# First units of a chunk scan prepared inside the projection's last item

## The chip, the cores and the metric

The kernel runs on one core of one Trainium2 chip. The metric is the device time of one execution in microseconds (us), as the median of several runs. TensorE is called PE in the profile, VectorE DVE, ScalarE ACT, GpSimd POOL and SyncE SP; ACTq and SPq are the instruction queues of ScalarE and SyncE that issue transfers.

## The reference

One step of a diffusion backbone with one layer, in float32, over 1024 sample tokens and 128 prompt tokens (nine chunks of 128). RMSNorm and modulation, one input projection of 1024 to 3600 columns, two head groups side by side, an output projection, then a gated convolutional MLP. The first group is a Hyena long convolution (four blocks of 128 channels). The second is an mLSTM with 4 heads of 128, scanned by chunks in two directions (d = 0 forward, d = 1 backward):

```python
def step(carry, xs):
    C, n, m = carry
    b = jnp.cumsum(lfc, axis=-1)
    dmat = jnp.where(causal, b[..., :, None] - b[..., None, :] + ic[..., None, :], -jnp.inf)
    inter = b + m[..., None]
    m_t = jnp.maximum(inter, jnp.max(dmat, axis=-1))
    s = einsum('bhtd,bhsd->bhts', qc, kc) * jnp.exp(dmat - m_t[..., None])
    w_inter = jnp.exp(inter - m_t)
    num = einsum('bhts,bhse->bhte', s, vc) + w_inter[..., None] * einsum('bhed,bhtd->bhte', C, qc)
    den = jnp.sum(s, axis=-1) + w_inter * einsum('bhd,bhtd->bht', n, qc)
    ...
    C_new = w_c * C + einsum('bhs,bhse,bhsd->bhed', w_s, vc, kc)
```

The prompt's scan starts from zero, the sample's from the inputs state_mlstm_C, n and m. Outputs are both token sets and the prompt's final states.

## The kernel before, in words

The program is a row of phases. A phase is a block in which each engine has a program of its own, written out by hand, with semaphores between them; all engines meet at a barrier at its end. Two phases matter here.

**The projection** (`project_and_hyena`, lines 398 to 1580) runs 32 items, one after another on TensorE. Each product is made in three passes (high x high, high x low and low x high part of float32, lines 231 to 235). Items 20 to 31 are "tokens" items: three token groups of 24 matmuls each, evicted by ScalarE (line 1294) to one of two stage buffers and stored by SyncE (`store`, line 723). Items 23 to 28 are the values v, 29 to 31 part of the output gate o, whose eviction is a Sigmoid. Beside the items run other works, tied to item numbers: the way back of the Hyena convolution (`transform_back`; `finish(c)` on VectorE, lines 1413 to 1428, makes block c from loads of hv and x0, issued by `load_block`, and SyncE stores it, `store_block`); the gates of the mLSTM (`gate_parts` on VectorE, `gate_exponents` on ScalarE, `gate_transfers` on SyncE); and at item 28 the output weights: ScalarE weighs them (lines 1319 to 1323) and takes the high part of the second half (line 1324), GpSimd the low part (line 991).

The gates end in rows that the scan needs spread over all partitions. At item 29, after VectorE's steps at lines 1510 to 1515, ScalarE makes four exponents (lines 1256 to 1259). SyncE then writes the rows to DRAM in 16 small stores (line 864), 2 for the output new_m (line 866), stores item 29 and the last Hyena block, and `load_rows_and_values` (line 815) loads them back, broadcast to 128 partitions (512 KB a unit: the tops and the inter weights, for the first 4 units), waits for the stores of items 27 and 28, and loads the values of the first 5 chunks (256 KB each, line 826). Item 30's store stands behind these. GpSimd, when mask and all 4 rows are there, makes the masked tops of units 0 and 1 (line 995). In the last item, n = 31, between its first and second token group, TensorE waits for the gates' diagonal (VectorE, line 1519, behind `finish(3)`) and for the last block, and transposes the gate columns (lines 1149, 1150). ScalarE issues the loads of the initial state behind item 30 (lines 1316 to 1318), in rows by value.

**The scan** (`chunk_scan`, lines 2176 to 2519) has 18 units (d, chunk, s, update): units 0 and 1 are the prompt's chunk in both directions (s = 0, zero state), then the sample's chunks alternate, forward from 0 and backward from 7. Units 2 to 9 meet a chunk for the first time. For a unit n:

- SyncE loads keys and queries of a chunk (`load_chunk`), and rows into a ring of 4 (`load_rows`);
- GpSimd adds the mask to the rows (`masked(n + 1)`, line 2386), then weights the queries (line 2398) and the values (line 2406);
- ScalarE takes exponentials (`decays`, line 2436, two units ahead) and copies transposed keys (`copy_keys`, line 2416);
- TensorE makes the scores (line 2328, one unit ahead), transposes the keys of a new chunk (line 2334), makes the numerators (line 2363 with the values, line 2364 with the state) and the state's update (line 2375);
- VectorE multiplies scores by decays (`probabilities`, line 2480), updates the state (line 2497) and makes the output (lines 2508 to 2516).

Ahead of the loop TensorE makes scores(0), transposes the first keys and the initial state (`turn_state`, line 2337), ScalarE makes decays(0), the key copy, decays(1) and the state's copies, VectorE probabilities(0).

## Time and profile before

| | us |
| --- | --- |
| median of 3 runs | 1619.41 |
| lowest and highest | 1618.31, 1622.28 |
| the profiled execution | 1622.19 |
| its span, first to last instruction | 1620.3 |
| projection's last item ends, scan's first product | 554.0, 564.39 |
| scan's last instructions, next phase's first product | 640.2, 640.90 |

Times in the rows below are microseconds from the span's start. A bracket at a row's end is the idle time of that engine ahead of it and what ended it. A row with xN merges N instructions of one line.

### The profile page before, as it was taken

To read this page: it belongs to the slowest core of one execution; us is meant where nothing else is said; L and a number is where in the kernel's file an instruction comes from. 1 tells how busy PE (TensorE), PEld (TensorE's weight loads), DVE (VectorE), ACT (ScalarE), POOL (GpSimd) and SP (SyncE) were. 2 spreads that over 40 slices of the span, in tenths; PEclk is the share of its full clock that TensorE was granted. 3 is DMA by queue.
4 is the path that set the end of the run, shared out by engine and by line. 5 is a ranking of instruction groups with operands and counts; after the bars stand their busy time and mean duration, and the time that the engine had idled before them with its cause. 6 is when DMAs were issued, how large, how long until landed. Compare 5 with 4: busy or idle time off the path is not lost.

```text
span 1620.3 us, 22641 instructions
## 1 busy us (share of the span) xinstructions
PE 1551.0 (96%) x9583; PEld 1431.7 (88%) x9583; DVE 988.4 (61%) x1369; ACT 487.4 (30%) x696; POOL 472.7 (29%) x212
## 2 busy tenths in 40 slices
PE   5889999999999798999899999999999999999997
PEld 1477899999999798999799999999999999999996
DVE  5657134788325457415788638855883787288846
ACT  2574123222442367434422102211221122022203
POOL 1665213211311286053323213222232221232210
PEclk9899999999999899999999999999999999999999
DMA  9753423433636786410101011010110101101102
GB/s 348 287 215 114 180 70 111 176 143 109 218 112 219 243 263 208 131 46 7 53 26 53 27 53 48 32 52 27 53 53 27 53 26 53 53 27 53 42 24 117
DMA packets 111207, 168.09 MB, mean 104 GB/s; under 512 B 6395, under 2 KB 88451, under 8 KB 105987
## 3 DMA queue, kind: packets, MB, share of 16 engines
q1 hardware_dynamic: 107983, 163.72, 29.4%
q10 hardware_dynamic: 3124, 2.93, 0.6%
q8 instruction: 76, 1.25, 0.3%
q14 instruction: 24, 0.20, 0.0%
HBM read 135.35 MB, written 31.27 MB: 103 GB/s over the span
## 4 chain that ended last, share of the span: by engine, by line
PE 57%; DVE 3%; ACT 1%; issue 0%; POOL 0%; ACTq 0%; DVEq 0%
PE psum L231 19%; PE psum L233 18%; PE psum L235 18%; DVE mlp_acc_a L3199 1%; DVE tail_scan_h L3079 1%; PE psum L3303 0%; PE psum L3463 0%; DVE mlp_h_lo L3085 0%; DVE w_raw L3268 0%; DVE mlp_h_lo L3073 0%; DVE mlp_acc_a L3268 0%; DVE tail_x L3223 0%; DVE mlp_h_lo L3130 0%; ACT tail_x L2976 0%; PE psum L3334 0%
## 5 line engine op out<-in xcount | busy, mean ns | idle before, releaser
L231 PE MATMUL psum<-mlp_h_hi,w_hi 128*128 128x384 f32 (+2 forms) x1248 | 305.3, 340 | 6.5 <-DVE mlp_acc_a L3199 3.5
L233 PE MATMUL psum<-mlp_h_lo,w_hi 128*128 128x384 f32 (+2 forms) x1248 | 301.3, 337 | 0.0
L235 PE MATMUL psum<-mlp_h_hi,w_lo 128*128 128x384 f32 (+2 forms) x1248 | 301.1, 336 | 0.0
L3199 DVE SCALAR_TENSOR_TENSOR w_raw<-psum,par,w_raw 128x945 f32<-128x945 f32 (+2 forms) x176 | 214.7, 1220 | 91.8 <-ACT w_raw L3020 88.0
L3199 DVE SCALAR_TENSOR_TENSOR mlp_acc_a<-psum,par,mlp_acc_a 128x945 f32<-128x945 f32 (+2 forms) x176 | 214.5, 1219 | 33.1 <-ACT mlp_acc_a L3020 29.9
L2791 POOL TENSOR_TENSOR w_lo<-w_raw,w_hi 128x2048 fp32r<-128x2048 f32 x32 | 148.1, 4627 | 288.4 <-ACT w_hi L2785 288.4
L231 PEld LDWEIGHTS psum<-mlp_h_hi,w_hi 128*128 128x128 f32 x1248 | 205.7, 189 | 25.5 <-issue 6.3
L233 PEld LDWEIGHTS psum<-mlp_h_lo,w_hi 128*128 128x128 f32 x1248 | 206.6, 189 | 15.3
L235 PEld LDWEIGHTS psum<-mlp_h_hi,w_lo 128*128 128x128 f32 x1248 | 206.3, 189 | 15.4
L3223 DVE SCALAR_TENSOR_TENSOR tail_x<-psum,mod,tail_x 128x384 f32<-128x384 f32 (+1 forms) x192 | 94.8, 515 | 128.3 <-PE psum L235 128.1
L233 PE MATMUL psum<-tail_g_lo,w_hi 128*128 128x384 f32 x480 | 160.3, 334 | 0.0
L235 PE MATMUL psum<-tail_g_hi,w_lo 128*128 128x384 f32 x480 | 160.3, 334 | 0.0
L231 PE MATMUL psum<-tail_g_hi,w_hi 128*128 128x384 f32 x480 | 160.3, 334 | 0.0
L231 PE MATMUL psum<-head_big_hi,w_hi 128*128 128x384 f32 (+3 forms) x578 | 146.6, 334 | 1.2 <-issue 1.2
L235 PE MATMUL psum<-head_big_hi,w_lo 128*128 128x384 f32 (+3 forms) x578 | 144.0, 330 | 0.0
L233 PE MATMUL psum<-head_big_lo,w_hi 128*128 128x384 f32 (+3 forms) x578 | 144.0, 330 | 0.0
L2894 POOL TENSOR_TENSOR tail_g_lo<-mlp_acc_a,tail_g_hi 128x1152 fp32r<-128x1152 f32 x20 | 53.8, 2690 | 250.4 <-ACT tail_g_hi L3033 250.4
L946 POOL TENSOR_TENSOR w_lo<-w_raw,w_hi 128x2048 fp32r<-128x2048 f32 (+1 forms) x13 | 60.3, 4639 | 195.6 <-ACT w_hi L1173 195.6
L231 PEld LDWEIGHTS psum<-head_big_hi,w_hi 128*128 128x128 f32 x578 | 97.9, 190 | 13.0 <-issue 6.5
L235 PEld LDWEIGHTS psum<-head_big_hi,w_lo 128*128 128x128 f32 x578 | 97.7, 190 | 7.2
L233 PEld LDWEIGHTS psum<-head_big_lo,w_hi 128*128 128x128 f32 x578 | 97.7, 190 | 7.1
L2785 ACT ACTIVATE w_hi<-w_raw 128x2048 fp32r<-128x2048 f32 x32 | 61.1, 1908 | 127.6 <-PE psum L235 127.6
(390 smaller groups left out, 2490.4 us busy)
## 6 DMA issues: line engine op xcount, KB each, us to landing
w_raw<-ffn_w_up SPq DMA_DIRECT2D x22, 1024.0 KB, 5.1
filt_ada<-ada_w SPq DMA_DIRECT2D x16, 1024.0 KB, 9.9
w_raw<-w_in SPq DMA_DIRECT2D x13, 1024.0 KB, 5.8
w_raw<-ffn_w_down SPq DMA_DIRECT2D x11, 1024.0 KB
scan_spread<-scratch_scan_rows SPq DMA_DIRECT2D x18, 512.0 KB, 5.9
rownorm_ada<-ada_w SPq DMA_DIRECT2D x8, 1024.0 KB, 6.7
rownorm_x<-x_sample SPq DMA_DIRECT2D x8, 512.0 KB, 5.4
scratch_kt<-kt_spec SPq DMA_DIRECT2D x4, 1024.0 KB, 3.8
```

What stands on the lines that cost most here:

```text
L231: ins = nc.tensor.matmul(out, wh, x_hi(k, i), start=begin, stop=False)
L233: ins = nc.tensor.matmul(out, wh, x_lo(k, i), start=False, stop=False)
L235: ins = nc.tensor.matmul(out, wl, x_hi(k, i), start=False, stop=end)
L946: nc.gpsimd.tensor_tensor(weight_part("lo", u), raw(u), weight_part("hi", u).bitcast(F32), ALU.subtract)\
L2785: nc.scalar.activation(w_hi[:, u % 2, :], w_raw, ACT.Copy).then_inc(w_hi_done, 1)
L2791: nc.gpsimd.tensor_tensor(w_lo[:, u % 2, :], w_raw, w_hi[:, u % 2, :].bitcast(F32), ALU.subtract).then_inc(w_lo_done, 1)
L2894: nc.gpsimd.tensor_tensor(lo, acc_a[:, j, :], hi.bitcast(F32), ALU.subtract).then_inc(g_lo_done, 1)
L3079: ins = stt(out=hacc[:, c, h, :], in0=hacc[:, c, h, :], scalar=ss[:, c, h:h + 1], in1=o[:, h, chunk_at(t)], op0=ALU.mult, op1=ALU.mult)
L3199: ins = stt(out=out, in0=image(up_at)[:, r0 + dy:r1 + dy, c0 + dx:c1 + dx], scalar=weight(i, loc, t), in1=out, op0=ALU.mult, op1=ALU.add)
L3223: ins = stt(out=out, in0=src[:, a:z], scalar=gate[:, j:j + 1], in1=out, op0=ALU.mult, op1=ALU.add)
```

## The change

Five things are done.

1. Into the projection's last item. TensorE, at the place where it transposes the gate columns, also transposes the first chunk's keys and makes its scores, once for units 0 and 1; all into banks 0 to 2, which item 30 has left, so that the wait for the last Hyena block (`finished`) moves from TensorE to VectorE. ScalarE, ahead of the last item's eviction, makes the decays of units 0 and 1 and the key copy; VectorE the probabilities of both. The scan begins with these in place.
2. ScalarE issues the five value loads, at item 28, ahead of the weighing of the output weights; it waits for the stores of items 27 and 28, and SyncE therefore stores item 28 first in that item.
3. SyncE loads rows for 3 units ahead (instead of 4), for units 0 and 1 only the tops (256 KB each); GpSimd's tops wait for those two and the mask. Item 30's store goes ahead of these loads, the new_m stores behind them.
4. The initial state is laid out by key in the kernel's input (a transposition of the input array), so one load in the scan puts C and n in place, and its transposes and copies go. Unit 3's rows are loaded in the scan. The SyncE order there is: second chunk, state, rows of unit 3, third and fourth chunk.
5. Units 0 and 1 leave out the product with the zero state and the weighting of its queries; some semaphores are shared.

```diff
@@ SyncE, projection @@
-            def load_rows_and_values():
-                sp.wait_ge(rows_out, 16 * (4 * HEADS + 2))
-                for n in range(SCAN_ROWS):
+            def load_first_rows():
+                sp.wait_ge(gate_out, 16 * (ENDS + STARTS + 4 * HEADS))
+                for n in range(ROWS_AHEAD):
                     d, c, s, up = SCAN_UNITS[n]
-                    src = dram["scan_rows"][d, c:c + 1]...
+                    parts = 2 if s else 1
+                    src = dram["scan_rows"][d, c:c + 1, 0:parts]...
...
+                if n == 28:
+                    store(n)
                 if 26 <= n < 29:
                     store_block(n - 26)
...
                 if n == 30:
                     store_block(CH - 1)
-                    load_rows_and_values()
-                if kind(n) in STORED:
+                if kind(n) in STORED and n != 28:
                     store(n)
+                if n == 30:
+                    load_first_rows()
+                    for d in range(2):
+                        sp.dma_start(io["new_m"]...)
@@ GpSimd, projection @@
-            pool.wait_ge(scan_rows_in, 16 * (1 + SCAN_ROWS))
+            pool.wait_ge(scan_rows_in, 16 * (1 + READY))
@@ TensorE, projection, last item @@
-                        pe.wait_ge(finished, CH)
+                        pe.wait_ge(evac, count(n - 1, "tokens"))
...
+                        pe.wait_ge(scan_in, 16 * 2)
+                        for h in range(HEADS):
+                            nc.tensor.transpose(ps[:, 1, ...], ahead["first_k"][:, h, :], mem["ident"][:]).then_inc(first_products, 1)
+                        for h in range(HEADS):
+                            nc.tensor.matmul(ps[:, 0, ...], ahead["first_k"][:, h, :], ahead["first_q"][:, h, :], ...)
@@ ScalarE, projection @@
+                if n == len(items) - 1:
+                    act.wait_ge(columns_made, 1)
+                    for i in range(READY):
+                        act.wait_ge(first_top, i + 1)
...
+                            ins = nc.scalar.activation(ahead["decay"][:, i, h, :], ahead["top"][:, i, h, :], ACT.Exp, ...)
+                    act.wait_ge(first_products, 1 + HEADS)
+                    act.wait_ge(y_out, 16 * (CH - 1))
+                    nc.scalar.activation(ahead["k_tok"][:, 0], ps[:, 1, :]..., ACT.Copy)
                 act.wait_ge(product_done, n + 1)
...
-                if n == 30:
-                    act.wait_ge(finished, CH)
-                    for d in range(2):
-                        act.dma_start(ahead["c_rows"][d], io["state_mlstm_C"]...)
-                    act.dma_start(ahead["n_rows"], io["state_mlstm_n"]...)
+                if n == 28:
+                    for i in range(27, 29):
+                        j = count(i, *STORED) - 1
+                        act.wait_ge(stored[j % ST], 32 * (j // ST + 1))
+                    act.wait_ge(back, 1 + 2 * CH)
+                    act.wait_ge(y_lo_done, 1 + 2 * CH)
+                    for c in SCAN_ORDER[0:VALUES_AHEAD]:
+                        act.dma_start(ahead["v"][:, c, :, 0:HD], dram["v"][c]...).then_inc(values_and_rows_in, 16)
                 if n == 28:
                     act.wait_ge(w_out_in, 32)
@@ VectorE, projection, last item @@
+                    dve.wait_ge(first_products, 1 + 2 * HEADS)
+                    dve.wait_ge(finished, CH)
+                    for i in range(READY):
+                        dve.wait_ge(first_decay, i + 1)
+                        tt(ahead["prob"][:, i], ps[:, 0, :]..., ahead["decay"][:, i], ALU.mult)
@@ SyncE, scan @@
-            for c in order[1:4]:
+            load_chunk(order[1])
+            sp.dma_start(C[:, 1], io["start_by_key"]...).then_inc(state_in, 16)
+            for n in range(ROWS_AHEAD, RB):
+                load_rows(n)
+            for c in order[2:4]:
                 load_chunk(c)
@@ TensorE, scan @@
-            scores(0)
-            turn_keys(order[0], 1)
-            turn_state()
             for n in range(N):
-                if n + 1 < N:
+                if READY <= n + 1 < N and n >= READY:
                     scores(n + 1)
...
+                    nc.tensor.matmul(wide(num, h), prob[:, n % 2, h, :], v[:, c, h, :], start=True, stop=not s)
+                    if s:
+                        ins = nc.tensor.matmul(wide(num, h), qw[:, n % 2, h, :], C[:, s, 4 * d + h, :], start=False, stop=True)
                 ins.then_inc(num_done, 1)
-                if n == 0:
-                    pe.wait_ge(c_copied, 3)
+                if n == READY - 1:
+                    scores(READY)
+                    turn_keys(units[READY][1], B_S + (READY - 1) % 2)
```

## Rows read from the trace of the kernel before

**Rows 1.** Stretches: length, busy of PE, PEld, DVE, ACT, POOL, clock, DMA share, GB/s.
```profile
554.00:557.00 3.00, 0.00 (x0) 0.00 (x0) 0.00 (x0) 0.81 (x1) 0.00 (x0) 0.92 1.00 351
...
564.30:573.30 9.00, 8.91 (x54) 8.59 (x55) 2.30 (x3) 6.72 (x18) 7.54 (x7) 0.67 0.90 275
573.30:585.00 11.70, 11.70 (x108) 11.70 (x106) 7.67 (x28) 6.38 (x24) 7.96 (x8) 1.00 1.05 328
```
**Rows 2.** Timeline of TensorE: start, us, engine, line, operation [idle before <- releaser].
```profile
547.58 0.49 PE L1149 MATMUL psum<-ident,front_gates 128*128 128x128 f32 x3
...
564.39 2.04 PE L2328 MATMUL psum<-scan_first_q,scan_first_k 128*128 128x128 f32 x8 [10.42 <-PEq L259]
...
573.30 1.05 PE L2328 MATMUL psum<-tail_x 128*128 128x128 f32 x8
...
577.31 1.05 PE L2328 MATMUL psum<-tail_x 128*128 128x128 f32 x8
...
587.20 0.60 PE L2334 MATMUL psum<-ident,tail_x 128*128 128x128 f32 x4
```
**Rows 3.** Timeline of GpSimd, from 533 to 585.
```profile
533.28 4.62 POOL L991 TENSOR_TENSOR w_lo<-w_raw,w_hi 128x2048 fp32r<-128x2048 f32 x1 [35.16 <-ACT w_hi L1324]
559.80 0.16 POOL L993 MEMSET scan_v<- 128x36 f32 x1 [21.91 <-DMA scan_spread<-scratch_scan_rows]
...
575.59 1.27 POOL L2386 TENSOR_TENSOR scan_top<-scan_spread,scan_mask 128x512 f32<-128x512 f32 x1 [0.56 <-DMA scan_spread<-scratch_scan_rows]
...
582.28 1.27 POOL L2386 TENSOR_TENSOR scan_top<-scan_spread,scan_mask 128x512 f32<-128x512 f32 x1 [3.18 <-DMA scan_spread<-scratch_scan_rows]
```
**Rows 4.** Waits of SyncE's queue around the barrier: total us, times, longest.
```profile
SPq L259 <- DMA scan_v<-scratch_v: 2.5, 1, 2.5
```
**Rows 5.** Timeline of ScalarE, items 28 to 31 and the scan's start.
```profile
527.93 3.32 ACT L214 ACTIVATE w_raw<-w_raw,par 128x256 f32<-128x256 f32 x8 [2.17 <-PE psum L235]
...
538.63 0.40 ACT L1256 ACTIVATE front_gates<-front_gates,hyi_gate_small 128x128 f32<-128x128 f32 x1 [5.42 <-DVEq L1516]
...
539.72 1.28 ACT L1294 ACT_TABLE_LOAD   x1
...
545.72 0.61 ACTq L1317 DMA_DIRECT2D scan_weighted_q<-state_mlstm_C  x1
...
554.00 0.81 ACT L1294 ACTIVATE head_stage<-psum 128x768 f32<-128x768 f32 x1 [8.25 <-PE psum L235]
...
565.75 1.26 ACT L2436 ACTIVATE scan_decay<-scan_top,front_gates 128x128 f32<-128x128 f32 x4
567.32 0.60 ACT L2416 ACTIVATE scan_k_tok<-psum 128x512 f32<-128x512 f32 x1 [0.31 <-PE psum L2334]
```
**Rows 6.** Timeline of VectorE: a gate step, the last Hyena block, the diagonal.
```profile
533.34 4.71 DVE L1511 TENSOR_TENSOR front_gates<-front_gates 128x128 f32<-128x128 f32 x1
...
540.28 0.82 DVE L1417 TENSOR_SCALAR hyi_value<-hyi_value,par 128x1152 f32<-128x1152 f32 x1 [1.74 <-DMA hyi_x<-scratch_x]
...
545.18 0.28 DVE L1519 TENSOR_SCALAR front_gates<-ident,hyi_gate_small 128x128 f32<-128x128 f32 x1
```
**Rows 7.** Timeline of SyncE's queue, items 27 to 30 (the us are those of issuing).
```profile
528.95 0.40 SPq L733 DMA_DIRECT2D scratch_v<-head_stage  x1
...
534.89 0.54 SPq L733 DMA_DIRECT2D scratch_v<-head_stage  x1
...
539.73 5.96 SPq L864 DMA_DIRECT2D scratch_scan_rows<-front_gates  x16
545.73 0.63 SPq L866 DMA_DIRECT2D new_m<-hyi_gate_chunks  x2
...
548.62 2.62 SPq L821 DMA_DIRECT2D scan_spread<-scratch_scan_rows  x4
551.34 8.49 SPq L826 DMA_DIRECT2D scan_v<-scratch_v  x5
```
**Rows 8.** The tile scratch_y: the block stores' and loads' time from issue to landing.
```profile
DMA to landing us min/median/max: 2.8/3.4/9.8
```

More of the change, by code:

```diff
@@ L365 @@
 VALUES_AHEAD = 5
+ROWS_AHEAD = 3
+READY = 2
 def scan_memory(nc, base):
@@ L926, in _ @@
                     store_block(CH - 1)
-                    load_rows_and_values()
-                if kind(n) in STORED:
+                if kind(n) in STORED and n != 28:
                     store(n)
+                if n == 30:
+                    load_first_rows()
+                    for d in range(2):
+                        sp.dma_start(io["new_m"][0, 0, d].rearrange("(h o) -> h o", o=1), after[ROWS_OF[d], NT - 1:NT])\
+                          .then_inc(gate_out, 16)
                 if n in (11, 13, 15):
@@ L991, in _ @@
             nc.gpsimd.tensor_tensor(mem["w_lo"][:, 1, :], mem["w_raw"][:, 1, :], mem["w_hi"][:, 1, :].bitcast(F32), ALU.subtract)
-            pool.wait_ge(scan_rows_in, 16 * (1 + SCAN_ROWS))
+            pool.wait_ge(scan_rows_in, 16 * (1 + READY))
+            for n in range(READY):
+                nc.gpsimd.tensor_tensor(ahead["top"][:, n], ahead["spread"][:, n, 0],
+                                        ahead["mask"][:, SCAN_UNITS[n][0], :].unsqueeze(1).broadcast_to([P, HEADS, P]), ALU.add)\
+                    .then_inc(first_top, 1)
             nc.gpsimd.memset(ahead["v"][:, :, :, HD:HD + 1], 1.0)
-            for n in range(2):
-                nc.gpsimd.tensor_tensor(ahead["top"][:, n], ahead["spread"][:, n, 0],
-                                        ahead["mask"][:, SCAN_UNITS[n][0], :].unsqueeze(1).broadcast_to([P, HEADS, P]), ALU.add)
         @blk.tensor
@@ L1275, in _ @@
                     gate_exponents(n)
+                if n == len(items) - 1:
+                    act.wait_ge(columns_made, 1)
+                    for i in range(READY):
+                        act.wait_ge(first_top, i + 1)
+                        d, c, _, _ = SCAN_UNITS[i]
+                        for h in range(HEADS):
+                            r = 64 * d + NT * h + c
+                            ins = nc.scalar.activation(ahead["decay"][:, i, h, :], ahead["top"][:, i, h, :], ACT.Exp, scale=-1.0,
+                                                       bias=mem["gates"][:, 6 * P + r:6 * P + r + 1])
+                        ins.then_inc(first_decay, 1)
+                    act.wait_ge(first_products, 1 + HEADS)
+                    act.wait_ge(y_out, 16 * (CH - 1))
+                    nc.scalar.activation(ahead["k_tok"][:, 0], ps[:, 1, :].rearrange("p (h d) -> p h d", h=HEADS), ACT.Copy)
                 act.wait_ge(product_done, n + 1)
@@ L1313, in _ @@
                     gate_exponents(n)
[L1314 to L1318 removed]
+                if n == 28:
[5 more added lines that the diff above has]
+                    for c in SCAN_ORDER[0:VALUES_AHEAD]:
+                        act.dma_start(ahead["v"][:, c, :, 0:HD], dram["v"][c].rearrange("p (h d) -> p h d", h=HEADS))\
+                            .then_inc(values_and_rows_in, 16)
                 if n == 28:
@@ L2276, in keys_before, with weighted_before, count_of, wait_unit @@
         def keys_before(n):
-            return sum(1 for c in order if first_unit[c] <= n)
+            return sum(1 for c in order[1:] if first_unit[c] <= n)
+        def weighted_before(n):
+            return sum(1 for i in range(n) if units[i][2])
+        def count_of(n):
+            return n - READY + 1
+        def wait_unit(eng, sem, n):
+            if n >= READY:
+                eng.wait_ge(sem, count_of(n))
         @blk.sync
@@ L2447, in set_h @@
                 ins.then_inc(set_done, 1)
-            nc.scalar.activation(first_exp[:], mem["ones"][:, 0:1], ACT.Exp)
-            decays(0)
-            copy_keys(0)
-            decays(1)
-            act.wait_ge(c_turned, 1)
-            for i in range(2):
-                nc.scalar.activation(C[:, 1, 4 * i:4 * i + 4, 0:HD], heads(B_C + i), ACT.Copy).then_inc(c_copied, 1)
-            nc.scalar.activation(C[:, 1, :, HD], ps[:, 5, 0:8], ACT.Copy).then_inc(c_copied, 1)
             for n in range(N):
```

160 lines of the change are left out of this document (73 added, 87 removed).

## The prediction

> **What bounds the kernel now.** I went first to the table of stretches around the hand-over from the projection to the scan [rows 1]. TensorE has nothing to do from the projection's end at 554.0; its clock averages 0.92 in the next 3 us, and the first 9 us of the scan run at a mean of 0.67 between its two levels. In the same stretches the DMA moves 275 to 351 GB/s, so the hand-over waits for transfers. TensorE's timeline [rows 2] gives the prices: the scan's first product starts at 564.39, the first product of unit 2 at 573.30, and from there a unit takes 577.31 - 573.30 = 4.01 us of gapless TensorE work. So two intervals can be won: the 10.4 us before 564.39, and whatever of the 8.9 us after it is preparation. Next, what ends the first interval: GpSimd waits 21.9 us for the broadcast rows, all there at 559.80, and then makes the masked tops [rows 3]; SyncE's final wait, 2.5 us, is for the value loads [rows 4]. Last, the engines that feed the rows [rows 5 to 7]: the 16 small row stores start at 539.73, when ScalarE has the exponents, and take 5.96 us to issue.
>
> **Part 1, ScalarE issues the value loads.** This is the step with a price. ScalarE begins to weigh the output weights at 527.93, after a wait for TensorE [rows 5]. In the new order it next waits until item 28's store has landed. That store moves ahead of the block store on SyncE, from 534.89 to about 529.4, right behind the previous one [rows 7]. The trace shows no landing for it; the block stores, half as large again, mostly land after 2.8 to 3.4 us [rows 8], and I take 3.2: ScalarE wakes at 532.6. Five issues of 256 KB follow. Below, one costs 0.61 us on ScalarE's own queue [rows 5]; above, the same five cost 8.49 us on SyncE behind a full queue [rows 7]. ScalarE's queue is empty then, so I take 0.61: 3.05 us, to 535.65. Weighing and high part last from 527.93 until GpSimd follows at 533.28 [rows 3, 5], 5.35 us, hence to 541.0, and the exponents (538.63 to 539.72, 1.1 us) to 542.1. The row stores therefore start 2.4 us **later** than now and end at 548.1.
>
> GpSimd's low part of the same weights moves with ScalarE, to 541.0 to 545.6 (4.62 us). Today it stands on VectorE's step of line 1511, which takes 4.71 us for 128x128 and ends as the GpSimd instruction ends [rows 3, 6]; that block goes, but ScalarE is by then the later one, so nothing is won. What the GpSimd instruction meets instead is the last Hyena block on VectorE, whose x0 load lands at 540.28 today [rows 6]. The value loads add 1.31 MB to the DMA at that time, 0 to 4.0 us at 328 GB/s [rows 1], so x0 lands between 540.3 and 544.3; for most of this interval GpSimd has already started, and VectorE stands still until 545.6. The block takes 540.28 to 545.18, 4.9 us, so it ends near 550.5, and the diagonal of the gates (0.28 us behind it) at 550.8. TensorE wants that diagonal at 547.58 [rows 2], so it stalls 3.2 us inside the projection's last item. That stall is not on the path: TensorE has 554.0 - 547.6 = 6.4 us of this item left, plus the new products (below), and even with its clock at the lower level for a few us it is done near 560.5.
>
> **Part 2, the rows.** SyncE ends the row stores at 548.1, stores item 29, waits for the last block (550.5), stores it and item 30, and issues the row loads at 551.5. Only parts of 256 KB are loaded for units 0 and 1. Ahead of them in the DMA are 0.98 MB of stores; with the two halves, 0.52 MB, that is 1.5 MB, 4.6 us at 328 GB/s, and about 0.7 us to the semaphore: the rows are there at **556.8** instead of 559.80 [rows 3]. The values were issued 16 us earlier and no longer end the phase; the new_m stores go behind the rows and are hidden while the block waits longer for ScalarE (if not, 0.63 us of issue [rows 7]).
>
> **Part 3, what stands between the rows and the barrier.** It is longer than now. Today 564.39 - 559.80 = 4.6 us. In the new order: the two tops (1.27 us each [rows 3]), the second unit's four exponentials (1.26), the key copy (0.60), the Sigmoid table (1.28), the last eviction (0.81) [rows 5], the store's issue (0.40 [rows 7]) and some 0.6 us of barrier, 7.5 us. The Exp table before them loads while ScalarE waits for the tops, and the probabilities on VectorE run beside the copy. The scan would start at 556.8 + 7.5 = 564.3: **0.1 us earlier**.
>
> The row of the table load says 1.28 us, with the next eviction able to follow at once. The Trainium skill, ScalarE: Activation LUTs, section What ACT_TABLE_LOAD costs, puts a switch at about 2.66 us with its drain; by that rule the sum, as an estimate, comes out 1.4 us worse.
>
> The products that move into the item are 4 transposes and 8 matmul passes, some 1.5 us at full clock (1.05 us for 8 passes [rows 2], the transposes at less than half of that); the path over the rows covers them as long as it ends after 560.5. If it doesn't, they cost 1.5.
>
> **Part 4, inside the scan.** Removed from its start: two score products (one, shared, is made before), the key transposes, nine state transposes, their copies, two decays and the half of units 0 and 1 that multiplies a zero state. TensorE could make unit 2's scores at about 5 us instead of 8.9. But the loads of the first units are late next: after the start, the state (0.53 MB, now loaded here) and unit 3's rows (0.52 MB, now loaded here) come on top of what is loaded today, 1.05 MB more, less 0.39 MB of item 30's store, which moved forward. Today GpSimd already waits for rows at 575.59 and 3.18 us at 582.28, that is 17.9 us after the start [rows 3]. 0.66 MB at 328 GB/s shift that to 19.9. Masking and the weighted queries, 1.27 us each, put unit 4's products at 22.4 us after the start. Today they stand behind the key transposes that start at 587.20 and take 0.60 [rows 2], at 23.4. From there both run at TensorE's pace. The gain is **1.0 us**. Bounds: with the DMA at 275 GB/s throughout [rows 1], the 5.9 MB up to unit 5's rows take 21.4 us, 22.0 with landing, and unit 4 comes 1.2 us later than today; if the loads never bind, unit 2's products start at 10.1 and unit 4's, two periods of 4.01 later, at 18.1, a gain of 5.3. I take 1.0 because GpSimd's wait for rows is in the trace, with the faster of the two rates beside it.
>
> **Sum.** 0.1 + 1.0 = 1.1 us less. The profiled execution took 1622.19 us (span 1620.3), so 1621.1; it lies 2.8 us above the median of the runs, 1619.41, and against that the forecast is 1618.3. A measurement of this kernel tells about 0.3% (4.9 us) from no change, so I forecast none that can be told.
>
> **Rivals.**
> *The loads keep up and the last block isn't blocked* (faster). If x0 lands before 541.0, only the block's last step waits for GpSimd, it ends near 547, the row loads wait only for the row stores (550.3), 1.37 MB of stores and 0.52 MB of rows end at 554.8, and the rows are there at 555.5: start 563.0, 1.4 us gained. With the scan's 5.3: 6.7, time 1612.7. For: from 553 on the new order has little left to move before the start. Against: GpSimd's waits for rows [rows 3], and the two conditions are independent; either alone gives 1617.0 or 1614.0.
> *ScalarE is held at its issues* (slower). The place is the five value loads; if they cost the 8.49 us that SyncE paid [rows 7], everything behind them on ScalarE comes 5.4 us later: exponents at 547.5, row stores to 553.5, their landing 2.2 us later (as from the end of the new_m issues, 546.36, to 548.62 [rows 7]), the stores ahead of the rows done at 558.5, rows at 560.8, start 568.3, 3.9 us later; less 1.0, the time is 1622.3. It decides from about 6.2 us of issue on: SyncE waits until 550.5 anyway, which hides the first 2 us. Against: 0.61 us on this queue [rows 5].
> *Nothing moves to the front* (no change). If the rows land after 557.9, the longer path behind them uses up all that the earlier loads give: 1619.4.
>
> **How the numbers follow.** Forecast, with its neighbours in which one of the two conditions holds weakly, 0.62; loads keep up, 0.16; ScalarE held, 0.12; nothing moves, 0.10. Below 1614.5 lie the first rival and a little of its neighbours: faster 0.17. Above 1624.3 lies only the worst of the second, with TensorE's stall reaching the path as well: slower 0.06. Same 0.77. The range runs from the first rival's time to the second's: 1612.7 to 1622.3.
>
> **What would show it.** Right: ScalarE's weighing starts near 535.6 and the exponents end near 542; line 1511 takes under 0.5 us; the last Hyena block ends near 550 with its first step stretched; TensorE has a gap of about 3 us at the columns' transposes; the tops start near 556.8; the scan's first product stands at 564, give or take 1.5; GpSimd waits for rows in units 3 to 5. Wrong: no gap in the last item and tops before 555.5; or unit 4's products less than 20 us after the start; or five issues of more than 1.2 us each.

## The result, and the profile after

The changed kernel is slower, by 0.4%: 1627.66 us, the median of 8 runs (1623.84 to 1629.91), beside 1621.36 of the kernel before on the same chip (8 runs, 1618.31 to 1622.32). The ratio is 1.0041, with a 95% interval from 1.0027 to 1.0054. The profiled execution took 1629.8, its span is 1627.6.

Of the difference between the two profiled executions, 0.56 us are there before the steps in question begin: item 28's eviction starts at 525.50 instead of 524.94, and over all profiled executions of this study it starts between 523.05 and 527.45. So below, positions are also given in us **from the start of item 28's eviction**, and called offsets. The scan's first product has the offset 39.45 before and 43.96 after (+4.5), the next phase's first product 115.96 and 122.75 (+6.8). The scan itself, from the one to the other, went from 76.51 to 78.79 (+2.3).

Stretches of the changed kernel (columns as in [rows 1]; the second and third begin with the scan, as the last two there):

```profile
557.00:560.00 3.00, 1.52 (x13) 1.32 (x12) 0.00 (x0) 0.00 (x0) 0.00 (x0) 1.00 0.75 238
569.40:578.40 9.00, 7.33 (x44) 7.17 (x44) 4.65 (x16) 4.19 (x10) 3.28 (x3) 0.74 0.97 272
578.40:590.00 11.60, 8.63 (x60) 8.42 (x61) 4.08 (x14) 4.60 (x17) 7.00 (x6) 0.85 0.98 295
```

Against the same stretches of [rows 1], TensorE lost its gapless work after unit 2: 8.63 busy of 11.60 us where there were 11.70 of 11.70, and the clock averages 0.85 there instead of 1.00. The DMA share is 0.97 and 0.98 (0.90 and 1.05 before), at 272 and 295 GB/s (275 and 328 before).

ScalarE's timeline, which answers to [rows 5]:

```profile
534.06 5.29 ACTq L1346 DMA_DIRECT2D scan_v<-scratch_v  x5
539.40 3.31 ACT L214 ACTIVATE w_raw<-w_raw,par 128x256 f32<-128x256 f32 x8 [13.09 <-issue]
...
545.35 0.28 ACT L1271 ACTIVATE hyi_gate_small<-hyi_gate_small 128x1 f32<-128x1 f32 x1
...
546.94 1.51 ACT L1319 ACTIVATE head_stage<-psum 128x768 f32<-128x768 f32 x2
561.95 1.28 ACT L1295 ACT_TABLE_LOAD   x1 [13.49 <-POOL scan_top L998]
563.24 2.44 ACT L1295 ACTIVATE scan_decay<-scan_top,front_gates 128x128 f32<-128x128 f32 x8
565.59 0.57 ACT L1300 ACTIVATE scan_k_tok<-psum 128x512 f32<-128x512 f32 x1
566.17 1.28 ACT L1319 ACT_TABLE_LOAD   x1
567.46 0.81 ACT L1319 ACTIVATE head_stage<-psum 128x768 f32<-128x768 f32 x1
```

The five value loads start at 534.06 and take 5.29 us. Weighing starts 11.5 us later than in [rows 5], the exponents end at 545.63 (offset 20.1 instead of 14.8). After 13.49 us of waiting for the tops ScalarE loads the Exp table *then*; decays, key copy, Sigmoid table and eviction follow one another until 568.27.

SyncE's, with [rows 7]:

```profile
545.65 6.11 SPq L862 DMA_DIRECT2D scratch_scan_rows<-front_gates  x16
...
552.25 1.54 SPq L828 DMA_DIRECT2D scratch_y<-hyi_x  x1
...
554.33 2.52 SPq L823 DMA_DIRECT2D scan_spread<-scratch_scan_rows  x3
...
568.30 0.41 SPq L734 DMA_DIRECT2D scratch_o<-head_stage  x1
```

The row stores follow the exponents at once, the row loads the row stores. The last item's store waits for ScalarE until 568.30; the barrier follows, and the scan's first product comes at 569.46.

GpSimd's, with [rows 3], and VectorE's, with [rows 6]:

```profile
544.74 4.55 POOL L995 TENSOR_TENSOR w_lo<-w_raw,w_hi 128x2048 fp32r<-128x2048 f32 x1 [46.06 <-ACT w_hi L1353]
560.61 2.48 POOL L998 TENSOR_TENSOR scan_top<-scan_spread,scan_mask 128x512 f32<-128x512 f32 x2 [11.32 <-DMA scan_spread<-scratch_scan_rows]
...
579.06 1.26 POOL L2426 TENSOR_TENSOR scan_top<-scan_spread,scan_mask 128x512 f32<-128x512 f32 x1 [5.78 <-DMA scan_spread<-scratch_scan_rows]
...
585.97 1.27 POOL L2426 TENSOR_TENSOR scan_top<-scan_spread,scan_mask 128x512 f32<-128x512 f32 x1 [3.41 <-DMA scan_spread<-scratch_scan_rows]
...
591.09 1.27 POOL L2426 TENSOR_TENSOR scan_top<-scan_spread,scan_mask 128x512 f32<-128x512 f32 x1 [1.61 <-DMA scan_spread<-scratch_scan_rows]
```

```profile
533.88 0.29 DVE L1539 TENSOR_TENSOR front_gates<-front_gates 128x128 f32<-128x128 f32 x1
...
545.04 5.46 DVE L1457 TENSOR_TENSOR hyi_x<-hyi_value,hyi_x 128x1152 f32<-128x1152 f32 x1
550.43 0.28 DVE L1547 TENSOR_SCALAR front_gates<-ident,hyi_gate_small 128x128 f32<-128x128 f32 x1
```

TensorE's, with [rows 2]:

```profile
547.80 0.38 PE L231 MATMUL psum<-w_hi,head_big_hi 128*128 128x256 f32 x1 [2.25 <-ACT head_stage L1319]
...
550.76 0.55 PE L1154 MATMUL psum<-ident,front_gates 128*128 128x128 f32 x3
...
569.46 2.06 PE L2400 MATMUL psum<-scan_v,scan_prob 128*128 128x129 f32 x8 [10.93 <-PEq L259]
...
580.57 1.85 PE L2374 MATMUL psum<-tail_x 128*128 128x128 f32 x8 [3.78 <-DMA tail_x<-scratch_q]
...
588.62 0.46 PE L2400 MATMUL psum<-scan_v,scan_prob 128*128 128x129 f32 x2 [0.80 <-POOL scan_weighted_q L2436]
...
593.85 0.46 PE L2400 MATMUL psum<-scan_v,scan_prob 128*128 128x129 f32 x2 [0.78 <-POOL scan_weighted_q L2436]
...
648.25 1.13 PE L3424 MATMUL psum<-ident,tail_scan_c 128*128 128x128 f32 x8 [3.71 <-PEq L259]
```

TensorE stalls 2.25 us ahead of item 31 for an eviction, and inside the scan 3.78 us for unit 3's queries. The tops of the kernel before, from which the chain T below counts:

```profile
559.88 2.48 POOL L995 TENSOR_TENSOR scan_top<-scan_spread,scan_mask 128x512 f32<-128x512 f32 x2
```

### The profile page after: what moved, and what is told of

Same layout as the page of the kernel before. It is cut to its first block, busy times and chain, and to the rows that moved or that the text cites. A ratio compares the mean times of both kernels' runs of the same rounds, so it can differ in the third digit from the quotient of the medians.

```text
span 1627.6 us, 22571 instructions
## 1 busy us (share of the span) xinstructions
PE 1549.7 (95%) x9550; PEld 1428.9 (88%) x9550; DVE 988.7 (61%) x1369; ACT 488.8 (30%) x694; POOL 469.8 (29%) x210
## 4 chain that ended last, share of the span: by engine, by line
PE 56%; DVE 3%; ACT 1%; issue 0%; POOL 0%; ACTq 0%; DVEq 0%
PE psum L231 19%; PE psum L233 18%; PE psum L235 18%; DVE mlp_acc_a L3225 1%; DVE tail_scan_h L3105 1%; PE psum L3329 0%; PE psum L3489 0%; DVE mlp_h_lo L3111 0%; DVE w_raw L3294 0%; DVE mlp_h_lo L3099 0%; DVE mlp_acc_a L3294 0%; DVE tail_x L3249 0%; DVE mlp_h_lo L3156 0%; ACT tail_x L3002 0%; PE psum L3360 0%
## 6 DMA issues: line engine op xcount, KB each, us to landing
filt_ada<-ada_w SPq DMA_DIRECT2D x16, 1024.0 KB, 10.3
```

## The experiments

Three theories came out of this comparison. **H**: ScalarE, held at the value loads, delays exponents, row stores, rows and scan. **T**: the chain behind the tops has become 4.3 us longer (8.85 from the tops to the first product, 4.51 before). **L**: state and unit 3's rows, loaded inside the scan, delay its first units. The rival **C**: the same bytes go through the same transfer engines, so who issues them, and when, changes nothing. **R** came up on the way: a gate step of VectorE takes 0.3 or about 4.6 us, depending on whether it starts ahead of GpSimd's low part of the output weights or behind it.

The table has the offsets of the profiled executions, the median, and the ratio to the kernel before on the same chip with its 95% interval.

| run | exponents end | row loads issued | tops start | first product | next phase | median us | ratio |
| --- | --- | --- | --- | --- | --- | --- | --- |
| before | 14.8 | 23.7 | 34.9 | 39.5 | 116.0 | | |
| after | 20.1 | 28.8 | 35.1 | 44.0 | 122.8 | 1627.66 | 1.0041 (1.0027 to 1.0054) |
| e1_sync | 14.9 | 22.4 | 30.2 | 39.0 | 117.2 | 1621.62 | 0.9997 (0.9985 to 1.0010) |
| e2_late | 9.7 | 21.2 | 30.4 | 39.3 | 117.1 | 1624.29 | 1.0024 (1.0012 to 1.0036) |
| e3_rows4 | 20.3 | 28.8 | 35.0 | 43.8 | 120.4 | 1624.72 | 1.0018 (1.0008 to 1.0029) |
| e4_evict_first | 19.0 | 27.5 | 33.6 | 41.8 | 119.9 | 1624.79 | 1.0022 (1.0011 to 1.0033) |
| e5_before_loads | 19.7 | 28.7 | 38.5 | 41.3 | 117.0 | 1626.38 | 1.0035 (1.0021 to 1.0048) |
| e6_combined | 9.7 | 22.5 | 27.2 | 36.4 | 112.1 | 1618.76 | 0.9987 (0.9978 to 0.9995) |
| e7_table_and_key | 19.1 | 27.5 | 33.6 | 40.7 | 119.0 | 1624.91 | 1.0022 (1.0008 to 1.0036) |
| e8_item29 | 9.6 | 22.9 | 27.6 | 36.5 | 114.1 | 1620.53 | 1.0000 (0.9991 to 1.0010) |
| e9_table_ahead | 10.3 | 23.1 | 28.2 | 35.3 | 110.5 | 1617.59 | 0.9981 (0.9969 to 0.9993) |
| e10_split_waits | 10.3 | 23.0 | 28.1 | 35.2 | 111.2 | 1616.95 | 0.9976 (0.9968 to 0.9985) |
| e11_before_split_waits | 10.2 | 21.8 | 32.8 | 37.3 | 113.6 | 1620.54 | 0.9994 (0.9985 to 1.0004) |
| e12_before_item29 | 14.6 | 24.3 | 34.4 | 37.2 | 113.2 | 1618.75 | 0.9990 (0.9979 to 1.0002) |

The kernel before had the medians 1621.62, 1620.43 and 1621.27 beside the three groups of runs e1 to e4, e5 to e8 and e9 to e12.

### e1_sync: SyncE issues the value loads again

```diff
@@ SyncE, load_first_rows, behind the row loads @@
+                for i in range(27, 29):
+                    sp.wait_ge(stored[...], ...)
+                for c in SCAN_ORDER[0:VALUES_AHEAD]:
+                    sp.dma_start(ahead["v"][:, c, :, 0:HD], ...)
@@ ScalarE @@
-                if n == 28:
...
-                    for c in SCAN_ORDER[0:VALUES_AHEAD]:
-                        act.dma_start(ahead["v"][:, c, :, 0:HD], ...)
```

> The changed kernel with one part undone: SyncE issues the five value loads again, behind the three row loads. Theory H (ScalarE is held: in the changed kernel its exponents end at 545.6 because it stands at the value loads from TensorE's item 28 on, and row stores, rows and tops follow): ScalarE weighs near 528 again, the exponents end near 539.7 as before the change, the row loads are issued near 548.5, the tops start near 552 instead of 560.6, and the scan's first product comes at 561 to 563 instead of 569.5, the time 1619 to 1621 instead of 1627.7. Rival C (contention: stores, rows and values are the same bytes, whoever issues them): the exponents come earlier but the start of the scan by less than 3 us (566.5 or later), since rows and values share the transfers; time 1625 to 1628. Theory T (the longer ScalarE work behind the tops): the path behind the tops stays 8.8 us long in any case.

The exponents end 5.2 us earlier and the first product comes 4.95 earlier; the ratio is 0.9997. The whole loss of the changed kernel is gone by this one edit, as far as the time can tell. H stands, but C has a part: of 6.4 us by which the row loads are issued earlier, 5.0 arrive at the tops. H's numbers were missed: the first product stands at 565.50, later than its 561 to 563 and 1 us ahead of C's 566.5, and the tops at 556.64 where it had 552. Nor does the rest of the change win anything here: it is all still in place, and the time is that of the kernel before. SyncE's timeline:

```profile
541.46 5.82 SPq L868 DMA_DIRECT2D scratch_scan_rows<-front_gates  x16
...
548.93 3.27 SPq L823 DMA_DIRECT2D scan_spread<-scratch_scan_rows  x3
552.30 5.79 SPq L829 DMA_DIRECT2D scan_v<-scratch_v  x5
```

The tops start 7.7 us after the first row load is issued; in the changed kernel it is 6.3. From the tops to the first product it stays 8.86, as T had it.

### e2_late and e8_item29: ScalarE issues them later

The value loads stay with ScalarE, but the edit of e2_late moves them behind item 30's eviction, and that of e8_item29, with 29 in the same place, behind item 29's:

```diff
-                if n == 28:
+                if n == 30:
                     for i in range(27, 29):
                         act.wait_ge(stored[...], ...)
```

> The changed kernel, but ScalarE issues the five value loads at item 30, behind that item's eviction, where it has nothing to do until the tops. Theory H: as with SyncE's issue, exponents near 539.7, and since SyncE's queue has only the rows and new_m, the scan starts at 559 to 562 and the time is 1617 to 1620. Rival C: start at 566 or later, time 1625 to 1628. If the order of the two queues alone matters (values ahead of rows in the transfers), this run's rows come later than those of the run with SyncE's issue, by up to 4 us.

> The changed kernel, but ScalarE issues the value loads at item 29 behind its eviction, where the transfers have a pause while the row stores are issued (0.22 of their capacity used), one item earlier than in the run with item 30. Theory H: the exponents as in the runs with SyncE's or item 30's issue, 9.7 or 15 after item 28's eviction. Theory C for the rest: in those two runs the rows took 7.7 and 9.3 from the issue of the first row load to the tops, 6.3 in the changed kernel, because the values went beside them; here the values are gone by then, the rows take 6.3 or less, the tops start 27.5 to 28.5 after item 28's eviction and the first product comes at 36.5 to 37.5; time 1619 to 1621. If C is wrong: tops at 30, first product at 39, as in the other two.

Neither holds the exponents. In e2_late they end at 9.7, but the tops start only at 30.4, 9.3 us after the issue of the row loads; in e8_item29 it is 4.7 us, and the tops start at 27.6. The stretches show why. First e2_late:

```profile
540.69:544.69 4.00, 4.00 (x36) 4.00 (x35) 3.90 (x5) 0.12 (x1) 0.00 (x0) 1.00 0.23 72
544.69:548.69 4.00, 4.00 (x37) 4.00 (x36) 0.96 (x4) 0.69 (x1) 0.00 (x0) 1.00 0.91 268
```

then e8_item29:

```profile
541.40:545.40 4.00, 4.00 (x36) 4.00 (x35) 3.86 (x5) 0.00 (x0) 0.00 (x0) 1.00 1.21 305
```

In e2_late the DMA share is 0.23 for 4 us, and then the values (issued from 544.71) compete with the rows (from 545.84). In e8_item29 the values fill that pause. So the place decides twice: ahead of the exponents the loads hold ScalarE, beside the row loads they take the rows' share. C as it was put falls: the same bytes from the same queue, one item apart, bring the first product 2.8 us apart. H repeats: with the loads at item 28 the exponents end at offsets of 19.0 to 20.3 in five executions, in the nine others at 9.6 to 10.3 or, where VectorE's gate step met GpSimd (R), at 14.6 to 14.9. e8_item29 came out as expected (36.5, 1620.53). The first product of e2_late, at 563.95, is 2 us later than H alone had it and 2 us earlier than C alone. The time of e2_late, 1624.29, lies nearer to C's 1625 than to H's 1620, and is worse than its profile lets expect: the profiled execution, 1622.11, is among its fastest. That stays open.

### e5_before_loads and e12_before_item29: part 2 alone, in the kernel before

```diff
@@ SyncE, load_rows_and_values @@
-                for c in SCAN_ORDER[0:VALUES_AHEAD]:
-                    sp.dma_start(ahead["v"]...)
@@ ScalarE @@
+                if n == 28:
+                    for i in range(27, 29):
+                        act.wait_ge(stored[...], ...)
...
+                        act.dma_start(ahead["v"]...).then_inc(scan_in, 16)
```

e12_before_item29 has 29 in place of 28. In both, item 28's store goes ahead of the block store, as in the change.

> The kernel before, with part 2 of the change alone: ScalarE issues the five value loads at item 28, ahead of the weighing, and item 28's store stands ahead of the block store. Times are counted from the start of item 28's eviction, since executions differ by a microsecond or two ahead of it; in the kernel before the exponents end 14.8 later and the scan's first product comes 39.5 later, in the changed kernel 20.2 and 44.0. Theory H (ScalarE held at the loads): exponents near 20, SyncE no longer pays the loads behind the rows, rows 4 to 5 later than before the change, the scan's first product at 43 to 44, time 1625 to 1626 beside 1621.5. Rival C (the transfers are the bound, and the values are out of their way early): the first product at 38 to 40, time 1619 to 1622.

> The kernel before with part 2 alone, but with the five value loads on ScalarE at item 29 behind its eviction. With the loads at item 28 the exponents ended 19.7 after item 28's eviction and the median stood 5 to 6 above the kernel before's. Theory H: the cost was the place and not the queue; here the exponents end near 9.7 or 14.8 as without the loads, SyncE's queue is free behind the rows, the barrier no longer waits for the values (from the tops to the first product 2.8 instead of 4.5), first product 1.7 to 4 earlier than in the kernel before, time 1617.5 to 1620. Rival (loads from ScalarE's queue are slower for the rows wherever they stand): 1623 or more.

ScalarE's timeline of e5_before_loads:

```profile
535.36 5.02 ACTq L1323 DMA_DIRECT2D scan_v<-scratch_v  x5
540.42 3.31 ACT L214 ACTIVATE w_raw<-w_raw,par 128x256 f32<-128x256 f32 x8 [12.67 <-issue]
...
546.37 0.28 ACT L1256 ACTIVATE hyi_gate_small<-hyi_gate_small 128x1 f32<-128x1 f32 x1
```

Part 2 alone delays the exponents by 4.9 us and the tops by 3.5, and makes the kernel before slower (1.0035). The first product came at 41.3, not at 43 to 44: with the values out of the way the barrier follows the tops after 2.8 us instead of 4.5. At item 29 the same five loads cost nothing: first product 37.2, ratio 0.9990 with an interval that still touches 1. In e5_before_loads the median lies further above the kernel before (about 5.9 us) than the offset of the next phase (1.0); the profiled execution was the fastest of its four, with 2.0 us of its time ahead of item 28's eviction (526.95), where the moved loads have no part. The slower ones were not profiled; why the time rose by so much more than the offsets stays open.

### e3_rows4: unit 3's rows loaded in the projection

```diff
-ROWS_AHEAD = 3
+ROWS_AHEAD = 4
```

> The changed kernel, but the rows of unit 3 (0.52 MB) are loaded in the projection again, behind those of units 0 to 2. Theory L (the scan's first 25 us are bound by its transfers; state and unit 3's rows were added there): TensorE's wait of 3.8 us ahead of unit 3's scores shrinks by 1.6 us or more and the scan, 78.8 us from its first to the next phase's first product, takes 77.2 or less; the start stays at 569.5, as the tops wait for the first two rows only; time 1626. Rival C: the bytes are the same, the barrier waits for them, the start comes 1.5 us later and nothing is won; 1627.7. Theory H and theory T say nothing on it.

```profile
570.22 2.06 PE L2400 MATMUL psum<-scan_v,scan_prob 128*128 128x129 f32 x8 [9.18 <-PEq L259]
...
578.59 1.16 PE L2374 MATMUL psum<-tail_x 128*128 128x128 f32 x8 [0.40 <-DMA tail_x<-scratch_q]
...
586.47 0.77 PE L2400 MATMUL psum<-scan_v,scan_prob 128*128 128x129 f32 x2 [2.27 <-POOL scan_weighted_q L2436]
```

TensorE's wait ahead of unit 3's scores fell from 3.78 to 0.40, the scan from 78.79 to 76.51, which is the length that it had before; the start did not move (offset 43.8). L holds, and in full: one load of 0.52 MB, moved out of the scan, is the scan's whole loss. Part of the wait moves on: the one for unit 3's weighted queries grew from 0.80 to 2.27. The length of the scan repeats: 77.6 to 78.8 in the six executions that load three rows ahead, 75.2 to 76.5 in the four that load four, 75.7 to 76.5 in the four of the kernel before and its variants. So the products, transposes and decays taken from the scan's start didn't make it shorter. The load costs nothing in the projection, since the barrier waits for ScalarE anyway.

### e4_evict_first and e7_table_and_key: the chain behind the tops

e4_evict_first puts the block with decays and key copy behind the last item's eviction. e7_table_and_key leaves the eviction, and changes ahead of the wait for the tops (the key copy behind the decays goes, and VectorE's waits for them count one more):

```diff
                 if n == len(items) - 1:
+                    act.wait_ge(first_products, 1 + HEADS)
+                    act.wait_ge(y_out, 16 * (CH - 1))
+                    nc.scalar.activation(ahead["k_tok"][:, 0], ...)
                     act.wait_ge(columns_made, 1)
+                    nc.scalar.activation(ahead["decay"][:, 0, 0, 0:1], mem["ones"][:, 0:1], ACT.Exp).then_inc(first_decay, 1)
+                    act.wait_ge(first_decay, 1)
                     for i in range(READY):
                         act.wait_ge(first_top, i + 1)
```

> The changed kernel, but ScalarE does the last item's eviction (Sigmoid) ahead of the decays and the key copy instead of behind them. Theory T (ScalarE's chain behind the tops sets the start: Exp table 1.28, eight decays 2.44, key copy 0.57, Sigmoid table 1.28, eviction 0.81, then the store's issue and the barrier): the eviction moves to about 559, the Sigmoid table load leaves the chain and the one at the scan's first decays goes as well; VectorE's second probabilities, which end near 566.8, are next; the scan starts 1.5 to 2.1 us earlier, near 567.7, time 1626. Rival (something else ends the phase: the store of the Hyena block, the value loads): the start stays at 569.5. Theory H: the exponents and the rows stay where they are, so the tops still start near 560.6.

> The changed kernel, in which ScalarE makes the key copy before it waits for the tops and takes one exponential of a single column there, so that the Exp table is loaded while it waits. Theory T: the Exp table load (1.28) and the key copy (0.57) leave the chain between the tops and the barrier, which falls from 8.85 to 7.0; the scan's first product 1.85 earlier, time 1625.8. Rival: the chain is bound by GpSimd's second top and VectorE's probabilities, and less than 0.6 is won.

ScalarE in e4_evict_first:

```profile
559.25 0.81 ACT L1306 ACTIVATE head_stage<-psum 128x768 f32<-128x768 f32 x1 [14.40 <-PE psum L235]
560.08 1.28 ACT L1315 ACT_TABLE_LOAD   x1
561.37 2.44 ACT L1315 ACTIVATE scan_decay<-scan_top,front_gates 128x128 f32<-128x128 f32 x8
```

and in e7_table_and_key:

```profile
550.60 1.28 ACT L1293 ACT_TABLE_LOAD   x1
551.89 0.20 ACT L1293 ACTIVATE scan_decay<-ones 128x1 f32<-128x1 f32 x1
559.45 2.44 ACT L1300 ACTIVATE scan_decay<-scan_top,front_gates 128x128 f32<-128x128 f32 x8 [7.35 <-POOL scan_top L998]
```

In the latter the decays begin with no table load between them and the top, and the chain from the tops to the first product falls from 8.85 to 7.10, by 1.75 where 1.85 was expected. T stands: these are costs of the path. The chain repeats too: 8.84 to 8.87 in the five executions that leave it alone, 7.10 to 7.15 in the three with this edit. In e4_evict_first it fell by 0.6 only: the decays then waited for TensorE's end and the eviction, 560.08, while the first top had been ready since 557.9. The expected 1.5 to 2.1 was a miss, because that wait was left out. (The first product came 2.2 earlier; 1.5 of that stands at the tops already.)

### e6_combined and e9_table_ahead: the repairs together

Both load the values at item 29 and rows for 4 units. e6_combined has the key copy first and the eviction ahead of the decays; e9_table_ahead has the edit of e7_table_and_key.

> The changed kernel with four edits: value loads issued by ScalarE at item 29 behind its eviction, rows of 4 units in the projection, the last item's eviction ahead of the decays, the key copy ahead of both. If H, T and L are separate and add: the scan's first product 36 to 37 after item 28's eviction (TensorE's end of the projection near 31.5, then eviction 0.81, Exp table 1.28, decays 2.44, probabilities and barrier about 2), the scan 76.5 long, time 1617 to 1619, below the kernel before (1621.5). If the transfers bind the rows whatever the order (C): the first product at 38.5 or later, time 1620 to 1622.

> The changed kernel with value loads at item 29, rows of 4 units in the projection, and the Exp table and the key copy ahead of the tops (the last item's eviction stays behind the decays). In the combined run before, the tops were there 27.2 after item 28's eviction, but the decays waited behind TensorE's end of the projection (30.2) and the eviction. Theory T: here decays end near 31.2, then Sigmoid table, eviction, store and barrier, 1.28 + 0.81 + 1.15: first product near 34.5, 1.9 earlier than in that run; scan 75.8 long; time 1616 to 1617.5. Rival: the barrier waits for the transfers (fourth row, new_m, stores) and not for ScalarE: first product at 36, time 1618.5 to 1619.

In e6_combined ScalarE is bound by TensorE's end:

```profile
554.33 0.60 ACT L1308 ACTIVATE scan_k_tok<-psum 128x512 f32<-128x512 f32 x1 [9.59 <-PE psum L235]
554.82 0.81 ACT L1310 ACTIVATE head_stage<-psum 128x768 f32<-128x768 f32 x1
555.64 1.28 ACT L1319 ACT_TABLE_LOAD   x1
556.94 2.44 ACT L1319 ACTIVATE scan_decay<-scan_top,front_gates 128x128 f32<-128x128 f32 x8
```

and in e9_table_ahead by the tops:

```profile
553.77 2.46 ACT L1300 ACTIVATE scan_decay<-scan_top,front_gates 128x128 f32<-128x128 f32 x8 [3.63 <-POOL scan_top L998]
556.25 1.28 ACT L1321 ACT_TABLE_LOAD   x1
```

The first products are at 36.4 and 35.3; both kernels are faster than before and after (0.9987 and 0.9981). The second won 1.1 of the 1.9 expected, since its rows came 1.0 later. The three costs are separate, and taking them away together gives what no single one gave. That the preparation in the last item has a share in this isn't shown: the kernel before gains 2.5 us by its median with the value loads at item 29 alone (e12_before_item29, 0.9990 against 0.9981, intervals that overlap). By the offsets of the next phase e9_table_ahead is 2.7 us ahead of it (110.5 against 113.2), but in the profiled execution of e12_before_item29 VectorE's gate step met GpSimd (exponents at 14.6), which is worth 2.3 of that offset in the kernel before (e11_before_split_waits below).

### e10_split_waits and e11_before_split_waits: who comes first, VectorE or GpSimd

```diff
             pool.wait_ge(w_out_hi, 1)
+            pool.wait_ge(gate_end, 1)
             nc.gpsimd.tensor_tensor(mem["w_lo"][:, 1, :], ...)
```

The first is e9_table_ahead with this line, the second the kernel before with it alone.

> The run with the table ahead, and GpSimd's low part of the output weights waits for VectorE's gate steps. In profiled executions VectorE's step right behind the third Hyena block comes 0.05 to 0.8 us before or after the start of this GpSimd instruction, and where it comes after, it takes 4.6 to 4.7 instead of 0.28 and the exponents end 5 later (14.8 against 9.7 after item 28's eviction). Theory R (this race goes either way from execution to execution, and some of the timed ones pay it): the profile is that of the run without the wait, the median falls by 0.5 to 2 and the spread narrows. Rival: the race always ends the same way in this kernel: no difference within 0.5.

> The kernel before, with GpSimd's low part waiting for VectorE's gate steps and nothing else. In its profile the step at line 1511 took 4.71 beside the GpSimd instruction. Theory R: the step takes 0.29, the exponents end near 10 after item 28's eviction instead of 14.8, the last Hyena block is not touched (its x0 lands 15.3 after the eviction, the GpSimd instruction ends near 13.5), the row loads are issued near 20.7 instead of 23.7, rows and scan start 2 to 3 earlier, time 1618.5 to 1619.5 beside 1621. Rival C: the rows land when the stores ahead of them are out: less than 1 won.

In e11_before_split_waits, VectorE's step and the GpSimd instruction (at line 1511 of [rows 6] it took 4.71):

```profile
535.64 0.29 DVE L1512 TENSOR_TENSOR front_gates<-front_gates 128x128 f32<-128x128 f32 x1
```

```profile
536.63 4.61 POOL L992 TENSOR_TENSOR w_lo<-w_raw,w_hi 128x2048 fp32r<-128x2048 f32 x1 [36.00 <-DVEq L1517]
```

The exponents end at 10.2 instead of 14.8, the first product comes 2.1 earlier, as R had it; the median fell by 0.7 only, where R had 1.5 to 2.5, with an interval that holds 1. In e10_split_waits the offsets are those of e9_table_ahead, the median is 0.6 lower, and its 11 runs lie between 1615.58 and 1618.39 where those of e9_table_ahead spread from 1612.35 to 1621.07. That fits R, but runs of e9_table_ahead were also faster than any of e10_split_waits, so that the race makes the spread is not shown. The ratio 0.9976 (0.9968 to 0.9985) is the best measured.

## Why the prediction was wrong

The forecast was 1618.3 and no change; the range ended at 1622.3, below every run of the changed kernel. Of the 7.9 us between the predicted and the measured position of the next phase (1.1 earlier against 6.8 later), 4.6 lie at the scan's start (3.25 at the rows, 1.35 behind them) and 3.3 inside it.

**Part 1, the price of the value loads: mis-sized.** ScalarE woke 0.9 us later than worked out (offset 8.56 against 7.66), and five issues took 5.29 us, not 3.05. "ScalarE's queue is empty then, so I take 0.61" is the sentence that failed: the shortest of the five took 0.59, the median one 0.81 and the last and longest 2.18, in a queue that held nothing else (why, no run shows); in the four other executions with these loads at item 28 the five took 5.11, 3.93, 5.02 and 5.39 (e3, e4, e5, e7), and at items 29 and 30 they took 3.6 to 5.7 in six: there they are not cheaper, the exponents only no longer wait for them. The exponents ended 3.0 later than forecast, the row loads were issued 2.3 later, the rows were there 3.25 later (offset 35.1 against 31.9). The rival in which ScalarE is held had the mechanism, with the chance 0.12. Its threshold of about 6.2 us doesn't follow from its sum: 3.05 and the 2 us that SyncE's wait for the last block hides make 5.05. Issues of 5.29 and a waking 0.9 later lie above that: the row stores ended at 551.76, behind the block (550.50), so that wait hid nothing any more.

Of what stood beside it, some came out: the step of line 1511 took 0.29, the GpSimd instruction met the last Hyena block, and TensorE ended the projection at 558.5, ahead of the tops, so the new products cost nothing. That the block ended at 550.50, where 550.5 was forecast, is luck: GpSimd came at 544.74, 3.7 us later than worked out, and met only the block's last step, not its first. The stall of TensorE was in another place, ahead of item 31 and for item 29's eviction, which also stands behind the loads.

**Part 2: right in kind.** The rows took 6.3 us from their issue, where 5.3 was worked out; the 0.7 us to the semaphore in that sum stand in no row, and the traces show only the whole. That the values "no longer end the phase" is right, and e2_late shows the other side: had they been issued beside the rows, they would have cost 2.8 us of the tops' start against e8_item29.

**Part 3, the chain behind the tops: a step was put into a wait that it doesn't use.** "The Exp table before them loads while ScalarE waits for the tops" is wrong: the load stands at 561.95, behind 13.49 us of idling. 7.5 forecast, 8.85 measured, and e7_table_and_key gives the load and the key copy back (1.75). The Trainium skill, ScalarE: Activation LUTs, section Step-by-step: what each stage is for, says that the compiler places the load right before the activation that needs it. The trace agrees; the prediction should have read that with the wait ahead of the activation. Of the 2.66 us which the same page, section What ACT_TABLE_LOAD costs, gives for a switch, the trace again shows 1.28, with the next instruction 0.01 behind.

**Part 4, inside the scan: the sign was wrong.** The loads were named as what is late next, but the gain was taken as 1.0 by the faster of two transfer rates. Measured is a loss of 2.3, beyond the bound of 1.2. The transfers ran at 272 and 295 GB/s in the first two stretches, under the 328 assumed. The sum followed one chain, from unit 5's rows to unit 4's products: the rows were there 21.6 us after the start (591.09) instead of 19.9, and the products came at 24.4 (593.85) instead of 22.4. In the kernel before they stand 23.25 after the start (587.64), so this is 1.1 of the loss, within the bound; the other 1.1 came behind that, where the prediction let both kernels run "at TensorE's pace". Unit 3's queries, behind the state and unit 3's rows on SyncE, came 3.78 us late, which the sum did not have; and TensorE, having idled, was granted a mean clock of 0.85 there, between the levels of 1.2 and 2.4 GHz (0.5 and 1): eight products took 1.85 us behind that wait, 1.05 in [rows 2]. e3_rows4 takes the loss away with one load.

**The chances.** Two unknown costs, the issues and the transfer rate, were taken at their better end; the slower rival has the worse end of the first alone. The errors were all of one sign, and each goes away by an edit of its own; the range should have held two of them at once.

## What to carry to other kernels

A load that moves to another engine's queue is not free there: it must be costed by its waits and its issues (3.6 to 5.7 us for these five) against the instructions behind it, and the best of the places tried here is where that engine has nothing due and the transfers pause (one item later, worth 7.5 us at the scan's start). In these traces a table load doesn't use a wait that stands directly ahead of its activation; a one-column activation ahead of the wait makes it do so (e7_table_and_key). And what is taken off a phase that ends in transfers must not come back as transfers at the next phase's start.

## What the runs showed of the hardware beyond that

A VectorE step of 0.28 to 0.29 us took 4.62 to 4.71 when it met the GpSimd subtraction of 128x2048, and did so or not by tenths of a microsecond: in e1_sync the step started 0.06 us behind the GpSimd instruction and took 4.64, in e2_late it started 0.8 ahead of it and took 0.28. For the exponents that is about 5 us (offsets of 14.8 and 10.2), for the scan's start 2.1 (e11_before_split_waits). In other runs the same instruction stretched a step of the last Hyena block to 5.46 (the changed kernel) or 5.56 (e4_evict_first, another step of it). The Trainium skill, SBUF — State Buffer, section Who interferes with whom, has it that the two engines share a pair of ports under an exclusive lock and that the order of issue decides who waits; the traces agree: in each of these cases the later one, VectorE, stood until GpSimd ended, and then did its work.
